# One rotation of the S5 scan written to SBUF through separate products instead of in place in PSUM

## The reference

```python
def s5_states(u, a_re, a_im, log_dt, b_re, b_im):
    ...
    mag = jnp.exp(dt * a_re)
    ang = dt * a_im
    abar_re, abar_im = mag * jnp.cos(ang), mag * jnp.sin(ang)
    ...
    x_re, x_im = cmul(f_re, f_im, bu_re, bu_im)
    a_shape = (1, u.shape[1]) + abar_re.shape
    _, _, h_re, h_im = lax.associative_scan(
        s5_combine,
        (jnp.broadcast_to(abar_re, a_shape), jnp.broadcast_to(abar_im, a_shape), x_re, x_im),
        axis=1)
    return h_re, h_im

def s5_mixer(hx, hc, ...):
    ...
        h_re, h_im = s5_states(u, a_re[di], a_im[di], log_dt[di], b_re[di], b_im[di])

        def readout(hr, hi):
            y = (jnp.einsum('btgp,gcp->btgc', hr, c_re[di].astype(jnp.float32))
                 - jnp.einsum('btgp,gcp->btgc', hi, c_im[di].astype(jnp.float32)))
            ...
    ...
    def glu(y):
        z = jax.nn.gelu(y)
        p = z @ glu_w + glu_b
        return p[..., :D_MODEL] * jax.nn.sigmoid(p[..., D_MODEL:])
```

## Time and profile before

| what | value |
|---|---|
| median of 3 runs | 2113.39 us (2113.13 to 2116.53) |
| the profiled execution: its own time / its span | 2116.53 us / 2114.7 us |
| mean granted TensorE clock | 0.971 of full |
| PE busy | 1974.8 us, 93% of the span |
| DVE busy | 1482.6 us, 70% |
| POOL busy | 589.1 us, 28% |
| S5 stretch, 505.3 to 596.2 us: length | 90.9 us |
| ... PE, DVE, ACT, POOL busy in it | 86.1, 62.7, 27.0, 61.8 us |

### The profile page before, as it was taken

How to read it: one execution, slowest core, us unless ns; L and a number is a source line. 1 busy time by engine, 2 the same in 40 slices (tenths; PEclk the granted TensorE clock), 3 DMA queues, 4 the chain that set the end, 5 groups by cost and what they waited for, 6 DMA issues and landing times.

```text
span 2114.7 us, 37558 instructions
## 1 busy us (share of the span) xinstructions
PE 1974.8 (93%) x14838; PEld 1671.6 (79%) x14838; DVE 1482.6 (70%) x2273; ACT 707.2 (33%) x1126; POOL 589.1 (28%) x465
## 2 busy tenths in 40 slices
PE   3999999997998999999989999998999999879997
PEld 0778778776986788888768888886888998779996
DVE  8968768757735985858989486358577777655555
ACT  2322222224333421222243122225455555426332
POOL 2245575553922120212412021140000000022113
PEclk8999999998999999999999999998999999989999
DMA  8365665655734354644425353222111111014553
GB/s 324 130 243 197 202 223 202 211 178 204 295 120 138 120 179 139 216 142 154 175 100 192 135 178 139 95 85 64 42 45 50 50 42 61 23 60 161 179 178 98
DMA packets 85633, 305.04 MB, mean 144 GB/s; under 512 B 9856, under 2 KB 21632, under 8 KB 76032
## 3 DMA queue, kind: packets, MB, share of 16 engines
q1 hardware_dynamic: 80896, 285.41, 39.5%
q0 software_dynamic: 2304, 9.44, 1.1%
q10 hardware_dynamic: 2304, 8.39, 1.0%
HBM read 275.94 MB, written 27.26 MB: 143 GB/s over the span
## 4 chain that ended last, share of the span: by engine, by line
PE 82%; DVE 9%; ACT 3%; issue 2%; POOL 2%; DVEq 1%; DMA 1%; SPq 0%; ACTq 0%; POOLq 0%
PE PS L228 41%; PE PS L219 6%; PE PS L221 6%; PE PS L220 6%; PE PS L1639 6%; PE PS L1652 6%; PE PS L1236 1%; DVE wlo L264 1%; PE PS L620 1%; DVE rstd L386 1%; PE PS L1071 1%; POOL hidl L603 1%; PE PS L1198 1%; PE PS L1218 1%; PE PS L1045 1%
## 5 line engine op out<-in xcount | busy, mean ns | idle before, releaser
L264 DVE TENSOR_TENSOR wlo<-raw,whi 128x1024 fp32r<-128x1024 f32 x314 | 479.0, 1566 | 80.9 <-ACT whi L258 79.2
L228 PE MATMUL PS<-hh,whi 128*128 128x512 f32 (+1 forms) x1536 | 443.9, 371 | 37.2 <-DVE hl L407 30.0
L228 PE MATMUL PS<-hl,whi 128*128 128x512 f32 (+1 forms) x1536 | 440.1, 368 | 0.0
L228 PE MATMUL PS<-hh,wlo 128*128 128x512 f32 (+1 forms) x1536 | 439.3, 368 | 0.0
L258 ACT ACTIVATE whi<-raw 128x1024 fp32r<-128x1024 f32 x300 | 301.3, 1052 | 277.6 <-PE PS L221 246.0
L228 PEld LDWEIGHTS PS<-hh,whi 128*128 128x128 f32 x1536 | 278.0, 191 | 92.4 <-issue 37.6
L228 PEld LDWEIGHTS PS<-hl,whi 128*128 128x128 f32 x1536 | 280.3, 191 | 47.2
L228 PEld LDWEIGHTS PS<-hh,wlo 128*128 128x128 f32 x1536 | 280.2, 191 | 47.1
L601 POOL CAST hidh<-gt 128x512 f32 (+2 forms) x88 | 62.0, 704 | 860.7 <-DVE gt L549 860.7
L219 PE MATMUL PS<-hidh,whi 128*128 128x512 f32 (+1 forms) x704 | 259.3, 368 | 12.7 <-POOL hidl L603 10.0
L221 PE MATMUL PS<-hidh,wlo 128*128 128x512 f32 (+1 forms) x704 | 256.6, 365 | 0.0
(11 more groups left out here) (336 smaller groups left out, 2755.5 us busy)
## 6 DMA issues: line engine op xcount, KB each, us to landing
modw<-in_mod_w SPq DMA_DIRECT2D x72, 1024.0 KB, 5.0
raw<-in_w_gdn SPq DMA_DIRECT2D x32, 512.0 KB, 4.1
cxd<-cx POOLq DMA_DIRECT2D x16, 576.0 KB, 3.8
cxS<-cxd SPq DMA_DIRECT2D x8, 1152.0 KB, 6.2
raw<-in_w_f0p0a SPq DMA_DIRECT2D x16, 512.0 KB, 6.9
vwd<-vws ACTq DMA_DIRECT2D x16, 512.0 KB, 6.5
raw<-in_w_f0p1a SPq DMA_DIRECT2D x16, 512.0 KB, 5.6
raw<-in_w_glu SPq DMA_DIRECT2D x16, 512.0 KB, 4.6
```

The lines of the kernel that those rows point to most:

```text
L228: ended = pe.matmul(dst, of[:, slot, c:c + P], moving, start=first and part_ == 0, stop=last and part_ == 2)
L264: dve.tensor_tensor(wlo[:, s, c], raw[:, s, c], whi[:, s, c].bitcast(F32), ALU.subtract)\
```

## The change

The rotation of V no longer writes back into PSUM. Both parts of the result go to a new use of SBUF space that was reserved but unused (`wr`), and all four products go to `ta` and `tb`, which are used twice. The two scans read `wr` instead of `PS`. `V_used` is given after the last combination, ahead of the scans, and the wait for the scans' results at the end of the block goes.

```diff
-        sb("wr_at", [P, 2, 8 * NK], F32, s5st)
+        wr = sb("wr", [P, 2, 8 * NK], F32, s5st)
...
+                wre, wim = (wr[:, r, :].rearrange("p (g k) -> p g k", k=NK) for r in range(2))
 
                 dve.tensor_tensor(ta[:, :, :], vr, ec, ALU.mult)
-                step(dve.tensor_tensor(tb[:, :, :], vi, ec, ALU.mult))
-                step(dve.tensor_tensor(vr, vr, es, ALU.mult))
-                step(dve.tensor_tensor(vi, vi, es, ALU.mult))
-                step(dve.tensor_tensor(vr, tb[:, :, :], vr, ALU.subtract))
-                step(dve.tensor_tensor(vi, ta[:, :, :], vi, ALU.add))
+                step(dve.tensor_tensor(tb[:, :, :], vi, es, ALU.mult))
+                step(dve.tensor_tensor(wre, ta[:, :, :], tb[:, :, :], ALU.add))
+                dve.tensor_tensor(ta[:, :, :], vi, ec, ALU.mult)
+                last = dve.tensor_tensor(tb[:, :, :], vr, es, ALU.mult)
+                step(last)
+                step(dve.tensor_tensor(wim, ta[:, :, :], tb[:, :, :], ALU.subtract))
+                dve.sem_inc(V_used, 1)
                 dve.wait_ge(H_zero, 2)
                 dve.wait_ge(ml_ready, b + 1)
                 if b >= 2:
                     dve.wait_ge(q_step, 6 * (b - 1))
                 for r in range(2):
-                    last = dve.tensor_tensor_scan(gr[s][:, r, :], mult, PS[:, 2 * s + 1 - r, :], 0.0, ALU.mult, ALU.add)
+                    last = dve.tensor_tensor_scan(gr[s][:, r, :], mult, wr[:, r, :], 0.0, ALU.mult, ALU.add)
                     last.then_inc(g_ready, 1)
-                dve.wait_ge(g_ready, 2 * b + 2)
-                dve.sem_inc(V_used, 1)
```

## The result

| | median | runs | ratio to before, 95% interval |
|---|---|---|---|
| before | 2111.95 us | 6 | |
| after | 2126.32 us (2123.42 to 2127.04) | 6 | 1.0059 [1.0047, 1.0072] |

By these medians the change costs 14.4 us; 14 were forecast, on a time before of 2113.4, which six runs now put at 2111.95. The ratio and its interval come from more runs: nine further ones of the changed kernel are on record (2121.3 to 2127.5), the profiled one among them. The median of all 15 is 2124.52, and the ratio 1.0059 is 12.5 us, 9.9 to 15.2 by the interval. So the cost is 12 to 14 us, and the forecast lies within what the runs can tell.

What follows compares the result with a forecast made beforehand. PE was taken as the bound, with POOL fully loaded close behind. POOL's 2.0 us later start plus 15.4 over six blocks, less about 3.1 in hand, gave +14.3, say +14: 2127.4 us against 2113.4, range 2117 to 2136.

Steps and rivals of the forecast that it cites:

- The price of a turn: POOL's loss beside DVE instructions with two SBUF operands: 0.4 us a combination, 0.88 a scan, 2.56 us a block.
- How often: DVE's blocks 2 to 7 beside POOL's blocks 1 to 6: 15.4 us; POOL's block 1 starts 2.0 us later.
- What POOL had in hand: POOL's lead over PE's readout of block 6: 3.1 us, to be taken off what POOL loses.
- next to nothing later takes the rest back: After PE's readout of block 6, the 14.3 us shift stays to the end; nothing later absorbs it.
- DVE itself ... no bound: DVE has 6.4 us of work in a 10.6 us block and waits for POOL up to four times 1.1: no bound.
- if POOL is slowed, nothing does: V_used ahead of the scans starts inputs(2) 2.5 us earlier; 0.8 us stays if POOL isn't slowed, nothing if it is.
- The clock: PE idles some 2 us a block; a fall behind the last wait can cost 1.5 us, at worst 3.5; 0 added.
- The signs: POOL's medians about 1.7 us, L1321, L1325 and scans 1 to 2.3, blocks 10.5 apart, PE waiting for POOL in most.
- Two readings of before: In the profile before: one pair of hl instructions beside POOL; a scan reads at under half the combinations' rate, 1.2 against 0.7 us.
- rival A: Scans don't take turns with POOL, only the combinations do: +2.3 us, 2115.7; chance 0.12.

Runs made afterwards that it cites:

- its control: The kernel before with POOL's turning forward of the states left out, each of its six instructions a block replaced by two that only write: 2112.06 us, 0.9998.

## Why the prediction was right, step by step

- **The price of a turn** was taken from one pair of instructions and one cast: 0.4 us a combination and 0.88 a scan, 2.56 us a block. Measured 0.39 and 0.86, 2.50 a block. That a scan, for which there was no row, behaves so was a bet, and the run with the scans alone is what settles it.
- **How often.** Six blocks were forecast. Five cost 2.5 us each. In block 5 POOL met two combinations and no scan (9.05 us instead of 10.27; the two hl instructions that it also met are there before as well), which is 0.65 us, and then it waited 2.28 us where it had waited 0.24. The two nearly cancel, so 15.4 forecast and 15.1 measured agree by luck in that part. The start of block 1 was +1.6 instead of +2.0.
- **What POOL had in hand**, 3.1 us at block 6, was right, and so was that next to nothing later takes the rest back: +13.8 at the readouts of blocks 6 and 7, +13.0 at the next norm. From there to the end the difference shrinks to 10.1, in stretches that the change does not touch; the kernel before and its control differ by as much there.
- **"DVE itself ... no bound" failed.** I counted DVE's waits at half their worst, 2.2 us a block. A scan follows a combination and the other scan at once, so POOL's next instruction always stands between them: the median scan takes 1.97 us, and DVE's blocks 4 and 5 come to 9.5 and 10.4 us instead of 6.4, waits of 3.1 to 4.0. With block 4 begun 2.4 us late behind the slow inputs(4), and with the GLU's two low parts behind block 5, DVE fell behind POOL. Without the slow inputs(4), in the run with more work for PE, POOL still waits 1.16 us.
- **"if POOL is slowed, nothing does", of the early V_used, failed too**: it is worth some 5 us within the changed kernel. For POOL's pace it is worth nothing, as I said; what I left out is that the GLU's first tile waits for the last V_used. inputs(2) did start early, but at 4.8 us from DVE's block 0, not 4.2, as PE was at its transposes until then.
- **The clock**: I took 2 us of idle time of PE in each block and added 0. In the profile PE waits in three blocks only, and the clock falls at block 1 and again at block 4, where the readout takes 5.38 us. These falls cost 0.8 us at POOL's block 6, by the run with more work for PE. Behind the last wait, where I had put 1.5 us and at worst 3.5, this profile shows none, while two experiments show 3.2. That the 0 held is luck as far as one profile can tell.
- **The signs.** POOL's blocks are 10.5 us apart, L1319 stays at 0.68 us, and the scans are at 1.97, as foretold. Not as foretold: POOL's medians are 1.51, 1.73 and 1.44 us and not all about 1.7, L1321 has a median of 0.75 us, and PE does not wait for POOL in most blocks.
- **Two readings of before were off** without changing the sum. Two pairs of hl instructions ran beside POOL, not one; the second, at 571.16 us, took 2.91 us. And a scan of 1.2 us against 0.69 reads at 57% of the rate, not at under half, which takes a little from rival A.

## What to carry to other kernels

Before moving operands of VectorE from PSUM to SBUF, look at what GpSimd does meanwhile. If it reads SBUF, each VectorE instruction that would have both inputs in SBUF costs it somewhat less than its own length (here 0.33 to 0.45 us for 0.69, 0.80 to 0.93 for 1.2), and costs VectorE up to one GpSimd instruction (here 1.1 us); the smallest duration of a line against its median and its largest shows such turns at a glance. An engine outside the chain with no idle time is the one to count first: what it loses, less what it has in hand, is the result, as long as it is what the others wait for in the end. Then look for what else waits on the slowed engine (here the GLU's first tile) and for what PE's clock does in its new pauses.

## What the runs showed of the hardware

- An instruction of DVE with one operand in PSUM and one in SBUF never waited for POOL (657 to 700 ns beside a busy POOL, before and after). With both in SBUF it did, whether it wrote to SBUF (up to 1805 ns, after) or to PSUM (up to 1809, the combinations alone).
- A scan with both operands in SBUF is no exception, although it takes 1.2 us for 512 elements against 0.69: it takes up to 2.23 us, and POOL's instruction beside it 2.06 to 2.19 instead of 1.27. With one operand in PSUM a scan stays at 1194 to 1221 ns.
- POOL's writes alone disturb nothing: 523 to 528 ns each, with DVE's combinations at 691 to 693 and its scans at 1198 to 1226.
- A combination takes 691 ns with both operands in SBUF and 686 to 695 with one in PSUM: SBUF as a source is not faster here.
- After PE had waited, between 1.0 and 4.1 us, its readouts often ran at the lower clock: 64 matmuls in up to 7.09 us at 0.50 instead of 3.79 at full. It was not so each time: the one behind the 1.26 us ahead of block 6, after the change, took 3.79.
